# Two layers of attention and a convolutional feed-forward on one core: the rotary key columns taken as one block of high and low halves, and the latents scaled before their transpose

## The chip, the cores and the metric

The kernel runs on one core of one Trainium2 chip. The metric is the device time of one execution in microseconds; lower is better. Three executions of the kernel before took 2210.03, 2210.46 and 2214.27 us, a median of 2210.46 us.

## The reference

For 256 tokens of width 2048 the reference computes two layers, each an attention mixer and a convolutional feed-forward, all in float32. The part around the change is the head of the first layer's mixer:

```python
def mla_mixer(h, positions, mem, w_in, q_norm, w_uq, kv_norm, w_ukv, mem_norm, w_mem_kv, w_o):
    proj = h @ w_in                                     # [256, 2048] @ [2048, 1600]
    q_lat, kv_lat, k_pe, q_mem = proj[..., :512], proj[..., 512:1024], proj[..., 1024:1088], proj[..., 1088:]
    q = (rms_norm(q_lat, q_norm) @ w_uq).reshape(b, s, 12, 192)
    q = concatenate([q[..., :128], rope(q[..., 128:], positions)], axis=-1)
    kv = (rms_norm(kv_lat, kv_norm) @ w_ukv).reshape(b, s, 12, 256)
    k_pe = rope(k_pe[:, :, None, :], positions)         # 64 columns, shared by the 12 heads
    ...
```

Here `h` is `rms_norm(x, a_attn_norm_pre)`, `rms_norm` divides each row by the root of its mean square and multiplies by a gain for each column, and `rope` rotates the two halves of the columns by an angle for each position.

## The kernel before

TensorE multiplies in a format of fewer mantissa bits (fp32r). To keep float32 accuracy every operand is cut in two, a high half (the value rounded) and a low half (the rest), and every product is three matmuls: high by high, low by high, high by low. Activations stand transposed (`xT_hi`, `xT_lo`), with the 2048 columns in 16 chunks of 128 partitions.

**Weights.** SyncE loads one step of weights at a time into a ring of four slots, `w_raw` (L350). ScalarE rounds it into `w_hi` (L1169), VectorE subtracts into `w_lo` (L1708), and TensorE waits for `lo_ready` ahead of each step (L489). SyncE waits for `lo_ready` of four steps ago before it loads a slot again, ScalarE for `step_used`, which TensorE raises at the end of each step. The order on each engine is written out by hand: `splits_to(s)` emits all splits up to step s, and what stands between two of these calls runs between those splits.

**The stage KVLAT.** The first layer's input projection is taken as QLAT (512 query latents, 8 steps), KVLAT (512 key and value latents and the 64 rotary key columns, 16 steps of one chunk, 576 columns of weights) and QMEM (512 memory queries, 8 steps). A chunk of KVLAT is nine matmuls: for each of two blocks of 128 tokens three of 512 columns with the activations stationary, and three for the rotary columns in mode "T", with the 64 weight columns stationary and 256 tokens moving, into `ps[0:64, 7]` (L500 to L512).

**The latents.** At the end of QLAT ScalarE and VectorE scale the two token blocks of PSUM into `lat[:, 0]` (L1292, L1900), ScalarE takes the sums of squares (L1191), and VectorE takes the root's inverse and multiplies an identity matrix by it into `diag` (L1729). After KVLAT TensorE multiplies `lat[:, 0]` by `diag` (`norm_group`, L604), which transposes and scales it at once. The same is done for the key and value latents in `lat[:, 1]`, with `diag_kv`, after QMEM.

**The rotary key columns.** After KVLAT ScalarE copies the 64 x 256 sums to `pe_raw` (L1301). TensorE transposes them after the second step of QMEM (`unrotated_transpose`, L654). VectorE, which waits for that (semaphore `unrotated`), scales them (L1913), rotates them (L1883 to L1890), doubles them (L1895), and only then goes on to the split of the fourth step of QMEM.

Of the kernel before, what the change touches and what calls it, by code (L numbers as in the profile page):

```python
# [22 lines left out]
P = 128  # L23
F32 = mybir.dt.float32
# [3 lines left out]
ALU = mybir.AluOpType  # L28
# [3 lines left out]
S = 256  # L32
# [17 lines left out]
R = 4  # L50
# [94 lines left out]
def program(nc, x_in, mem_in, positions, inv_freq, w, vec, out):  # L145

    with ExitStack() as ctx:
# [46 lines left out]
        diag_kv = at("diag_kv", [P, TT, P], F32, H0 + 24 * KB)  # L194
# [271 lines left out]
        def _(pe):  # L466
# [6 lines left out]
            def product(s0, steps, tile_no, xhi, xlo, parts, width=512, chunks=2, per=0, i=None,  # L473
# [11 lines left out]
                for k, parts_now in turns:  # L485
# [8 lines left out]
                    for c in range(chunks):  # L494
# [5 lines left out]
                        for mode, bank, o0, on, tok, cols in parts_now:  # L500
                            rows = RD if bank >= 4 else P
                            dst = ps[0:rows, bank if bank >= 4 else pair + bank, o0:o0 + on]
# [4 lines left out]
                            pairs = [(a_hi, cols(wh)), (a_hi, cols(wl)), (a_lo, cols(wh))]  # L507
                            if mode == "T":
                                pairs = [(b, a) for a, b in (pairs[0], pairs[2], pairs[1])]
                            for q, (st, mv) in enumerate(pairs):  # L510
                                mm = nc.tensor.matmul(dst, st, mv, start=first and q == 0,  # L511
                                                      stop=last and q == 2, skip_group_check=True)  # L512
# [85 lines left out]
            def norm_group(src, g, diag=diag, tiles=range(TT)):  # L598


                for c in range(2):
                    for t in tiles:
                        f0 = (2 * g + c) * P
                        mm = nc.tensor.matmul(ps[:, 4 + g % 4, 256 * c + P * t:256 * c + P * t + P],  # L604
                                              src[:, t, f0:f0 + P], diag[:, t, :],
                                              start=True, stop=True, skip_group_check=True)
                if TT - 1 in tiles:
                    mm.then_inc(tr_ready, 1)

            def norm_transpose(src, chunks, diag_no, diag=diag):  # L610
                phase_free()
                pe.wait_ge(diag_ready, diag_no)
                for g in range(chunks // 2):
                    if g >= 4:
                        pe.wait_ge(tr_lo, done["N"] + g - 3)
                    norm_group(src, g, diag)
                done["N"] += chunks // 2

            def plain_transpose(src, g, tiles):
# [6 lines left out]
                return mm  # L626

# [238 lines left out]
            def x_group(g):  # L866
                if g >= 4:
# [8 lines left out]
            kpe_parts = [("T", 7, 0, 256, every, (lambda a: a[:, LORA:KVW]))]  # L876
            product(KVLAT, KC, KVLAT_T, xT_hi, xT_lo, n_parts() + kpe_parts, width=KVW, chunks=1)
            norm_transpose(lat[:, 0], 4, 2)
            product(QMEM, DSTEPS, QMEM_T, xT_hi, xT_lo, t_parts(),
                    after=lambda k: k == 1 and unrotated_transpose(6, 0, RD, 1))  # L880
            norm_transpose(lat[:, 1], 4, 3, diag_kv)
# [259 lines left out]
        def _(act):  # L1141
# [175 lines left out]
            to_turn(pe_raw[0:RD, 0, :], ps[0:RD, 7, 0:S])  # L1317
# [352 lines left out]
        def _(dve):  # L1670
# [11 lines left out]
            def split(s, per=0, i=None):  # L1682

                width = 1024
                if i is None and KVLAT <= s < QMEM:
                    width = KVW

# [9 lines left out]
                if i is None and gain_in_split(s):  # L1697
                    for c in range(2):
                        if s < CHUNKED:
# [8 lines left out]
                nc.vector.tensor_tensor(w_lo[:, s % R, 0:width], w_raw[:, s % R, 0:width],  # L1708
                                        w_hi[:, s % R, 0:width].bitcast(F32), ALU.subtract)\
# [23 lines left out]
            def norm(parts, dst=diag):  # L1733
                count["sq"] += 1
                dve.wait_ge(sq_ready, count["sq"])
                sums(parts)
                inverse_std()
                diagonal(dst)
# [159 lines left out]
            def latent_epilogue(k, t, s_end, dst):  # L1898
# [3 lines left out]
                norm(1, dst)  # L1902

            splits_to(KVLAT + AHEAD)
            latent_epilogue(0, QLAT_T, KVLAT, diag)
            splits_to(QMEM + AHEAD)
            latent_epilogue(1, KVLAT_T, QMEM, diag_kv)
# [4 lines left out]
            for t in range(TT):  # L1912
                d = nc.vector.tensor_scalar(raw[:, P * t:P * t + RD], ps[:, 6, P * t:P * t + RD],  # L1913
                                            rstd[:, t:t + 1], None, ALU.mult)
            link(d)
# [472 lines left out]
```

## Time and profile before

| | |
|---|---|
| three executions | 2210.03, 2210.46, 2214.27 us |
| the profiled execution | 2210.6 us, of which the span from first to last instruction is 2208.8 us |
| TensorE clock granted over the span | 0.999 of full speed |
| stage KVLAT | about 131 to 159 us of the span |
| stage QMEM | about 160.5 to 184 us of the span |

Times in rows are microseconds from the start of the span, durations of one instruction nanoseconds. PE is TensorE's matmul, PEld its weight load, DVE VectorE, ACT ScalarE, SPq the queue of SyncE. Matmuls are pipelined: the duration of one is longer than the distance to the next, so the distances between starts tell the pace, not the durations.

### The profile page before, as it was taken

The page shows a single profiled execution, that of the slowest core. Times are in us where ns is not written, and L with a number is a line of the kernel's source. Part 1 is how long each engine was busy: PE and PEld are TensorE (multiplying, and loading weights), DVE is VectorE, ACT ScalarE, POOL GpSimd, SP SyncE. Part 2 cuts the span into 40 slices and gives each one's busy share as a digit, 9 for nine tenths or more (in the row PEclk, how much of TensorE's full clock was granted, in tenths as well). Part 3 has the DMA queues.
Part 4 walks back from the last instruction along what each step waited for, and adds up shares of the span by engine and source line. Part 5 has one row for each costly group of instructions (what it writes and reads, how often), then busy time and mean ns, then how long its engine had stood idle before and what let it go on. Part 6 is the DMA issues. An engine that isn't in the chain of part 4 may idle for free.

```text
span 2208.8 us, 33764 instructions
## 1 busy us (share of the span) xinstructions
PE 2193.8 (99%) x12137; PEld 1909.2 (86%) x12137; DVE 1419.9 (64%) x1897; ACT 1224.1 (55%) x1697; POOL 3.9 (0%) x16
## 2 busy tenths in 40 slices
PE   9999999999999999999999999999999999999998
PEld 9989988888888888888888889888888888888887
DVE  6556656677777776545476667567767776774444
ACT  6655555666565656434465557556655665564443
POOL 0000000000000000000000000000000000000000
PEclk9999999999999999999999999999999999999999
DMA  8565345565656666656655654555565666566664
GB/s 282 180 181 163 115 124 171 182 190 185 197 179 187 192 195 202 202 182 204 195 172 182 197 166 125 182 171 179 188 187 183 195 183 197 179 218 200 192 192 151
DMA packets 208370, 405.61 MB, mean 184 GB/s; under 512 B 12877, under 2 KB 16327, under 8 KB 207519
## 3 DMA queue, kind: packets, MB, share of 16 engines
q1 hardware_dynamic: 207711, 400.29, 58.1%
q0 software_dynamic: 576, 4.19, 0.5%
q8 instruction: 54, 0.88, 0.2%
q14 instruction: 29, 0.24, 0.0%
HBM read 402.34 MB, written 2.10 MB: 183 GB/s over the span
## 4 chain that ended last, share of the span: by engine, by line
PE 98%; DVE 1%; ACT 0%; DMA 0%; issue 0%; DVEq 0%; ACTq 0%
PE ps L511 49%; PE ps L540 29%; PE ps L548 15%; PE ps L981 1%; PE ps L624 1%; PE ps L680 0%; PE ps L764 0%; PE ps L735 0%; PE ps L682 0%; PE ps L644 0%; PE ps L741 0%; DVE w_lo L1702 0%; PE ps L705 0%; DMA gain_rows<-in_gains 0%; PE ps L604 0%; DVE x L2072 0%
## 5 line engine op out<-in xcount | busy, mean ns | idle before, releaser
L1708 DVE TENSOR_TENSOR w_lo<-w_raw,w_hi 128x1024 fp32r<-128x1024 f32 (+1 forms) x636 | 763.3, 1211 | 510.6 <-ACT w_hi L1169 506.1
L1169 ACT ACTIVATE w_hi<-w_raw 128x1024 fp32r<-128x1024 f32 (+1 forms) x636 | 657.4, 1046 | 472.5 <-PE ps L511 337.9
L540 PE MATMUL ps<-xT,w_hi 128*128 128x512 f32 x2816 | 673.4, 391 | 0.1
L540 PEld LDWEIGHTS ps<-xT,w_hi 128*128 128x128 f32 x2816 | 517.1, 188 | 100.2 <-issue 0.4
L548 PEld LDWEIGHTS ps<-xT,w_lo 128*128 128x128 f32 x2816 | 361.6, 191 | 14.3 <-DVE w_lo L1708 0.4
L548 PE MATMUL ps<-xT,w_lo 128*128 128x256 f32 x2816 | 367.4, 283 | 0.0
L511 PE MATMUL ps<-w_hi,hT_hi 128*128 128x512 f32 x704 | 274.0, 389 | 0.0
L511 PE MATMUL ps<-w_hi,hT_lo 128*128 128x512 f32 x704 | 273.9, 389 | 0.0
L511 PE MATMUL ps<-w_lo,hT_hi 128*128 128x512 f32 x704 | 273.9, 389 | 0.0
L1702 DVE SCALAR_TENSOR_TENSOR w_lo<-w_raw,gcol,w_hi 128x512 fp32r<-128x512 f32 x224 | 156.1, 748 | 73.3 <-ACT w_hi L1163 73.2
L511 PE MATMUL ps<-w_hi,xT 128*128 128x512 f32 x640 | 202.2, 391 | 0.0
L1163 ACT ACTIVATE w_hi<-w_raw,gcol 128x512 fp32r<-128x512 f32 x224 | 148.6, 718 | 75.0 <-PE ps L511 63.7
L511 PEld LDWEIGHTS ps<-w_lo,hT_hi 128*128 128x128 f32 x704 | 132.2, 188 | 27.5
L511 PEld LDWEIGHTS ps<-w_hi,hT_hi 128*128 128x128 f32 x704 | 132.2, 188 | 27.4
L511 PEld LDWEIGHTS ps<-w_hi,hT_lo 128*128 128x128 f32 x704 | 132.2, 188 | 27.3
L511 PEld LDWEIGHTS ps<-w_hi,xT 128*128 128x128 f32 x640 | 120.1, 188 | 24.6
L511 PE MATMUL ps<-w_lo,xT 128*128 128x512 f32 x320 | 124.7, 390 | 0.0
L511 PE MATMUL ps<-w_hi,xbT_hi 128*128 128x512 f32 x256 | 100.6, 393 | 0.4 <-DVE w_lo L1702 0.4
L511 PE MATMUL ps<-w_hi,xbT_lo 128*128 128x512 f32 x256 | 99.8, 390 | 0.0
L511 PE MATMUL ps<-w_lo,xbT_hi 128*128 128x512 f32 x256 | 99.7, 389 | 0.0
L1551 ACT ACTIVATE hT_hi<-scratch 128x1024 f32 x22 | 23.4, 1062 | 97.3 <-DVE scratch L2206 97.3
L2196 DVE SCALAR_TENSOR_TENSOR scratch<-u_value,conv,scratch 128x255 f32<-128x255 f32 (+1 forms) x176 | 73.2, 478 | 3.2
(267 smaller groups left out, 2218.6 us busy)
## 6 DMA issues: line engine op xcount, KB each, us to landing
w_raw<-in_ffn_w_in SPq DMA_DIRECT2D x352, 512.0 KB, 4.2
w_raw<-in_ffn_w_out SPq DMA_DIRECT2D x176, 512.0 KB, 4.6
w_raw<-in_shared_w_kv SPq DMA_DIRECT2D x48, 512.0 KB, 3.9
w_raw<-in_a_w_o SPq DMA_DIRECT2D x32, 512.0 KB, 4.6
w_raw<-in_b_w_in SPq DMA_DIRECT2D x32, 512.0 KB, 4.8
w_raw<-in_b_w_o SPq DMA_DIRECT2D x32, 512.0 KB, 4.6
w_raw<-in_a_w_mem_kv SPq DMA_DIRECT2D x16, 512.0 KB, 6.9
w_raw<-in_b_w_mem_kv SPq DMA_DIRECT2D x16, 512.0 KB, 4.6
```

Source lines behind the costliest of these rows:

```text
L511: mm = nc.tensor.matmul(dst, st, mv, start=first and q == 0, stop=last and q == 2, skip_group_check=True)
L540: mm = nc.tensor.matmul(ps[:, base + m4, :].rearrange("p (a n) -> p a n", a=2), w_hi[:, slot, cols], xT[:, :, 2 * k + c, :], start=k == c ...
L548: mm = nc.tensor.matmul(ps[:, base + m4, S:2 * S], w_lo[:, slot, cols], xT_hi[:, 2 * k + c, :], start=False, stop=stop and c == 1, skip_gr ...
L624: mm = nc.tensor.transpose(ps[:, 4 + g % 4, o0:o0 + P], src[:, t, f0:f0 + P], ident[:, :])
L981: mm = nc.tensor.matmul(ps[:, pair + t, :], x_part[:, 2 * k + c, tok_t[t]], w_part[:, slot, 512 * c:512 * (c + 1)], start=t not in started ...
L1163: a = nc.scalar.activation(w_hi[:, s % R, cols], w_raw[:, s % R, cols], ACT.Copy, scale=gcol[:, row:row + 1])
L1169: nc.scalar.activation(w_hi[:, s % R, 0:width], w_raw[:, s % R, 0:width], ACT.Copy)\
L1551: nc.scalar.activation(hT_hi[:, bass.ds(i * 4, 4), :], scratch[:, 1], ACT.Copy).then_inc(h_hi, 1)
L1702: d = nc.vector.scalar_tensor_tensor(out=w_lo[:, s % R, cols], in0=w_raw[:, s % R, cols], scalar=gcol[:, row:row + 1], in1=w_hi[:, s % R, ...
L1708: nc.vector.tensor_tensor(w_lo[:, s % R, 0:width], w_raw[:, s % R, 0:width], w_hi[:, s % R, 0:width].bitcast(F32), ALU.subtract)\
L2196: d = nc.vector.scalar_tensor_tensor(out=c, in0=u, scalar=conv[:, layer, 2 - shift, bass.ds(ch, 1)], in1=c, op0=ALU.mult, op1=ALU.add)
```

## The change

Three things are changed in the first layer; the rest is as it was. In KVLAT, VectorE writes the low half of the 64 rotary columns not into `w_lo` but into `w_hi`, right of the high half (columns 576 to 640), with an instruction of its own. The two halves side by side are one stationary block of 128 columns, which is multiplied by the high and by the low activations (mode "halves"): two matmuls in place of three. The sums of the high half then stand in partitions 0 to 63 of bank 7 and those of the low half in 64 to 127, so that `pe_raw` has 128 rows, and after the transpose VectorE scales both and adds the second to the first. The latents are scaled in place by VectorE (`scale_latent`) and transposed plainly against the identity (`latent_transpose`); `diag_kv` goes. This is the whole difference:

```diff
--- before.py
+++ after.py
@@ -191,7 +191,6 @@
         vm_a = at("vm_a", [P, 2, MH, P], F32, H0 + 68 * KB)
         qpT = at("qpT", [P, AH // 2, S], F32, H0 + 72 * KB)
         kpT = at("kpT", [P, 2, S], F32, H0 + 78 * KB)
-        diag_kv = at("diag_kv", [P, TT, P], F32, H0 + 24 * KB)
 
         xbT_hi = at("xbT_hi", [P, KC, S], F32R, H0)
         xbT_lo = at("xbT_lo", [P, KC, S], F32R, H0 + 16 * KB)
@@ -498,18 +497,22 @@
                         ch = (first_chunk + n_ch) % (steps * chunks)
                         seen = set()
                         for mode, bank, o0, on, tok, cols in parts_now:
-                            rows = RD if bank >= 4 else P
-                            dst = ps[0:rows, bank if bank >= 4 else pair + bank, o0:o0 + on]
+                            dst = ps[:, bank if bank >= 4 else pair + bank, o0:o0 + on]
                             first = n_ch == 0 and bank not in seen
                             seen.add(bank)
                             last = n_ch == steps * chunks - 1
                             a_hi, a_lo = xhi[:, ch, tok], xlo[:, ch, tok]
-                            pairs = [(a_hi, cols(wh)), (a_hi, cols(wl)), (a_lo, cols(wh))]
+                            if mode == "halves":
+                                both = cols(w_hi[:, slot])
+                                pairs = [(both, a_hi), (both, a_lo)]
+                            else:
+                                pairs = [(a_hi, cols(wh)), (a_hi, cols(wl)), (a_lo, cols(wh))]
                             if mode == "T":
                                 pairs = [(b, a) for a, b in (pairs[0], pairs[2], pairs[1])]
                             for q, (st, mv) in enumerate(pairs):
                                 mm = nc.tensor.matmul(dst, st, mv, start=first and q == 0,
-                                                      stop=last and q == 2, skip_group_check=True)
+                                                      stop=last and q == len(pairs) - 1,
+                                                      skip_group_check=True)
                         if between and c + 1 < chunks:
                             between(k)
                     if not single or parts_now[0] is parts[-1]:
@@ -595,27 +598,6 @@
                 if items_done[0]:
                     pe.wait_ge(o_lo, items_done[0])
 
-            def norm_group(src, g, diag=diag, tiles=range(TT)):
-
-
-                for c in range(2):
-                    for t in tiles:
-                        f0 = (2 * g + c) * P
-                        mm = nc.tensor.matmul(ps[:, 4 + g % 4, 256 * c + P * t:256 * c + P * t + P],
-                                              src[:, t, f0:f0 + P], diag[:, t, :],
-                                              start=True, stop=True, skip_group_check=True)
-                if TT - 1 in tiles:
-                    mm.then_inc(tr_ready, 1)
-
-            def norm_transpose(src, chunks, diag_no, diag=diag):
-                phase_free()
-                pe.wait_ge(diag_ready, diag_no)
-                for g in range(chunks // 2):
-                    if g >= 4:
-                        pe.wait_ge(tr_lo, done["N"] + g - 3)
-                    norm_group(src, g, diag)
-                done["N"] += chunks // 2
-
             def plain_transpose(src, g, tiles):
 
                 for c in range(2):
@@ -624,6 +606,14 @@
                         mm = nc.tensor.transpose(ps[:, 4 + g % 4, o0:o0 + P], src[:, t, f0:f0 + P],
                                                  ident[:, :])
                 return mm
+
+            def latent_transpose(src, scaled_no):
+
+                phase_free()
+                pe.wait_ge(diag_ready, scaled_no)
+                for g in range(2):
+                    plain_transpose(src, g, range(TT)).then_inc(tr_ready, 1)
+                done["N"] += 2
 
             def x_transpose(g, tiles):
 
@@ -873,12 +863,12 @@
             product(QLAT, DSTEPS, QLAT_T, xT_hi, xT_lo, n_parts(),
                     late=[(k, None, tr_lo, base_n + k + 1) for k in range(DSTEPS)])
 
-            kpe_parts = [("T", 7, 0, 256, every, (lambda a: a[:, LORA:KVW]))]
+            kpe_parts = [("halves", 7, 0, 256, every, (lambda a: a[:, LORA:KVW + RD]))]
             product(KVLAT, KC, KVLAT_T, xT_hi, xT_lo, n_parts() + kpe_parts, width=KVW, chunks=1)
-            norm_transpose(lat[:, 0], 4, 2)
+            latent_transpose(lat[:, 0], 2)
             product(QMEM, DSTEPS, QMEM_T, xT_hi, xT_lo, t_parts(),
-                    after=lambda k: k == 1 and unrotated_transpose(6, 0, RD, 1))
-            norm_transpose(lat[:, 1], 4, 3, diag_kv)
+                    after=lambda k: k == 1 and unrotated_transpose(6, 0, P, 1))
+            latent_transpose(lat[:, 1], 3)
             rope_transpose(6, [rot[:, P * t:P * (t + 1)] for t in range(TT)], 1)
             qpe_blocks = [rot[:, P * t:P * (t + 1)] for t in range(TT)]
             for j in range(6):
@@ -1314,7 +1304,7 @@
             latent_epilogue(0, QLAT_T, KVLAT)
             splits_to(QMEM + AHEAD)
             latent_epilogue(1, KVLAT_T, QMEM)
-            to_turn(pe_raw[0:RD, 0, :], ps[0:RD, 7, 0:S])
+            to_turn(pe_raw[:, 0, :], ps[:, 7, 0:S])
             split_transposes(4, [(GAIN_ROWS["q_norm"], latq_hi)])
             splits_to(UQ + AHEAD)
             act.wait_ge(step_used, UQ)
@@ -1681,10 +1671,6 @@
 
             def split(s, per=0, i=None):
 
-                width = 1024
-                if i is None and KVLAT <= s < QMEM:
-                    width = KVW
-
                 if i is not None or s >= CHUNKED:
                     dve.wait_ge(hi_ready, val(s + 1, per, i))
                 if i is None and UQ <= s < UKV:
@@ -1705,8 +1691,15 @@
                             op0=ALU.mult, op1=ALU.subtract)
                     d.then_inc(lo_ready, 1)
                     return
-                nc.vector.tensor_tensor(w_lo[:, s % R, 0:width], w_raw[:, s % R, 0:width],
-                                        w_hi[:, s % R, 0:width].bitcast(F32), ALU.subtract)\
+                if i is None and KVLAT <= s < QMEM:
+                    for dst, cols in ((w_lo[:, s % R, 0:LORA], slice(0, LORA)),
+                                      (w_hi[:, s % R, KVW:KVW + RD], slice(LORA, KVW))):
+                        d = nc.vector.tensor_tensor(dst, w_raw[:, s % R, cols],
+                                                    w_hi[:, s % R, cols].bitcast(F32), ALU.subtract)
+                    d.then_inc(lo_ready, 1)
+                    return
+                nc.vector.tensor_tensor(w_lo[:, s % R, :], w_raw[:, s % R, :],
+                                        w_hi[:, s % R, :].bitcast(F32), ALU.subtract)\
                     .then_inc(lo_ready, 1)
 
             def splits_to(s):
@@ -1730,12 +1723,15 @@
                                                 ALU.mult)
                 d.then_inc(diag_ready, 1)
 
-            def norm(parts, dst=diag):
+            def scale_latent(k):
                 count["sq"] += 1
                 dve.wait_ge(sq_ready, count["sq"])
-                sums(parts)
+                sums(1)
                 inverse_std()
-                diagonal(dst)
+                for t in range(TT):
+                    d = nc.vector.tensor_scalar(lat[:, k, t, :], lat[:, k, t, :],
+                                                nrm[:, 4 + t:5 + t], None, ALU.mult)
+                d.then_inc(diag_ready, 1)
 
             def split_transposes(chunks, targets, following=None, start=3):
 
@@ -1895,16 +1891,16 @@
                     d = nc.vector.tensor_copy(rows[:, :, width:2 * width], rows[:, :, 0:width])
                 d.then_inc(rope_ready, 1)
 
-            def latent_epilogue(k, t, s_end, dst):
+            def latent_epilogue(k, t, s_end):
                 dve.wait_ge(step_used, s_end)
                 nc.vector.tensor_scalar(lat[:, k, 1, :], ps[:, 2 * (t % 2) + 1, :], rstd[:, 1:2], None,
                                         ALU.mult).then_inc(pair_dve, 1)
-                norm(1, dst)
+                scale_latent(k)
 
             splits_to(KVLAT + AHEAD)
-            latent_epilogue(0, QLAT_T, KVLAT, diag)
+            latent_epilogue(0, QLAT_T, KVLAT)
             splits_to(QMEM + AHEAD)
-            latent_epilogue(1, KVLAT_T, QMEM, diag_kv)
+            latent_epilogue(1, KVLAT_T, QMEM)
             split_transposes(4, [(GAIN_ROWS["q_norm"], latq_hi, latq_lo)])
             nc.vector.memset(kpT[RD:P, 0, :], 0.0)
             nc.vector.memset(kpT[0:RD, 1, :], 0.0)
@@ -1912,6 +1908,11 @@
             for t in range(TT):
                 d = nc.vector.tensor_scalar(raw[:, P * t:P * t + RD], ps[:, 6, P * t:P * t + RD],
                                             rstd[:, t:t + 1], None, ALU.mult)
+            link(d)
+            for t in range(TT):
+                d = nc.vector.scalar_tensor_tensor(
+                    out=raw[:, P * t:P * t + RD], in0=ps[:, 6, P * t + RD:P * (t + 1)],
+                    scalar=rstd[:, t:t + 1], in1=raw[:, P * t:P * t + RD], op0=ALU.mult, op1=ALU.add)
             link(d)
             rotate(unrotated, 1, P, RD, 0, RD // 2, twice=True)
             splits_to(UQ + AHEAD)
```

TensorE, one chunk of KVLAT. `ps` is the accumulator, `xT` the activations; left of the comma after the arrow are the operands of the matmul, and the last number is its output. Before:

```order
L511 MATMUL ps<-w_hi,xT 128x512
L511 MATMUL ps<-xT,w_hi 64x256 x2
L511 MATMUL ps<-xT,w_lo 64x256
L511 MATMUL ps<-w_hi,xT 128x512
L511 MATMUL ps<-w_lo,xT 128x512
L511 MATMUL ps<-w_hi,xT 128x512 x2
```

And after, at the same place:

```order
L513 MATMUL ps<-w_hi,xT 128x512
L513 MATMUL ps<-xT,w_hi 128x256 x2
L513 MATMUL ps<-w_hi,xT 128x512
L513 MATMUL ps<-w_lo,xT 128x512
L513 MATMUL ps<-w_hi,xT 128x512 x2
```

The three matmuls that write 64 partitions became two that write 128; the six of 512 columns around them stay.

VectorE at the start of KVLAT, from the first three splits through the query latents to the further splits (`nrm` is the sum of squares and the root's inverse). Before:

```order
L1708 TENSOR_TENSOR w_lo<-w_raw,w_hi 128x576 x3
L1900 TENSOR_SCALAR lat<-ps,rstd 128x512
L1719 TENSOR_REDUCE nrm<-ssp 128x2
L1725 RECIPROCAL nrm<-nrm 128x2
L1729 TENSOR_SCALAR diag<-ident,nrm 128x128 x2
L1708 TENSOR_TENSOR w_lo<-w_raw,w_hi 128x576 x13
```

After:

```order
L1697 TENSOR_TENSOR w_lo<-w_raw,w_hi 128x512
L1697 TENSOR_TENSOR w_hi<-w_raw,w_hi 128x64
L1896 TENSOR_SCALAR lat<-ps,rstd 128x512
L1712 TENSOR_REDUCE nrm<-ssp 128x2
L1718 RECIPROCAL nrm<-nrm 128x2
L1732 TENSOR_SCALAR lat<-lat,nrm 128x512 x2
L1697 TENSOR_TENSOR w_lo<-w_raw,w_hi 128x512
L1697 TENSOR_TENSOR w_hi<-w_raw,w_hi 128x64
```

Each of the 16 splits became two instructions, and the two scalings ahead of the fourth split have 512 columns in place of 128.

VectorE in QMEM, from the wait for the transposed rotary columns to the split of QMEM's fourth step (`scratch` holds them). Before:

```order
L1910 MEMSET kpT 64x256
L1913 TENSOR_SCALAR scratch<-ps,rstd 128x64 x2
L1883 TENSOR_TENSOR scratch<-scratch,sine 128x2x32
L1886 TENSOR_TENSOR scratch<-scratch,sine 128x2x32
L1887 TENSOR_TENSOR scratch<-scratch,cosine 128x2x32
L1888 TENSOR_TENSOR scratch<-scratch,cosine 128x2x32
L1889 TENSOR_TENSOR scratch<-scratch 128x2x32
L1890 TENSOR_TENSOR scratch<-scratch 128x2x32
L1895 COPY scratch<-scratch 128x2x64
L1708 TENSOR_TENSOR w_lo<-w_raw,w_hi 128x1024 x5
```

After:

```order
L1906 MEMSET kpT 64x256
L1909 TENSOR_SCALAR scratch<-ps,rstd 128x64 x2
L1913 SCALAR_TENSOR_TENSOR scratch<-ps,rstd,scratch 128x64 x2
L1879 TENSOR_TENSOR scratch<-scratch,sine 128x2x32
L1882 TENSOR_TENSOR scratch<-scratch,sine 128x2x32
L1883 TENSOR_TENSOR scratch<-scratch,cosine 128x2x32
L1884 TENSOR_TENSOR scratch<-scratch,cosine 128x2x32
L1885 TENSOR_TENSOR scratch<-scratch 128x2x32
L1886 TENSOR_TENSOR scratch<-scratch 128x2x32
L1891 COPY scratch<-scratch 128x2x64
L1701 TENSOR_TENSOR w_lo<-w_raw,w_hi 128x1024 x5
```

Two instructions came in between the scaling and the rotation, ahead of the five splits.

## Rows read from the trace of the kernel before

**Rows 1.** The profile's page: busy time of engines, and the chain that ended last.

```profile
PE 2193.8 (99%) x12137; PEld 1909.2 (86%) x12137; DVE 1419.9 (64%) x1897; ACT 1224.1 (55%) x1697; POOL 3.9 (0%) x16
...
PE 98%; DVE 1%; ACT 0%; DMA 0%; issue 0%; DVEq 0%; ACTq 0%
```

**Rows 2.** Timeline of TensorE in KVLAT: start, length, instruction; two merged are x2.

```profile
135.97 0.40 PE L511 MATMUL ps<-xT,w_hi 128*64 128x256 f32 x2
136.21 0.28 PE L511 MATMUL ps<-xT,w_lo 128*64 128x256 f32 x1
136.32 0.40 PE L511 MATMUL ps<-w_hi,xT 128*128 128x512 f32 x1
...
137.71 0.40 PE L511 MATMUL ps<-xT,w_hi 128*64 128x256 f32 x2
```

**Rows 3.** Instructions grouped by form: rotary matmuls and weight loads, busy us, mean ns.

```profile
L511 PEld LDWEIGHTS ps<-xT,w_hi 128*128 128x128 f32 x128 | 19.9, 192 | 0.2 <-DVE w_lo L1708 0.2
...
L511 PE MATMUL ps<-xT,w_hi 128*64 128x256 f32 x32 | 6.3, 280 | 0.0
...
L511 PEld LDWEIGHTS ps<-xT,w_hi 128*64 128x64 f32 x32 | 4.3, 134 | 2.1
```

**Rows 4.** The chain that ended last in time order: start, length, pieces, 85 to 100.

```profile
95.84 0.44 PE ps L624 x4
```

**Rows 5.** The same chain, 158 to 190: the latents' transposes and QMEM.

```profile
159.02 1.78 PE ps L604 x16
160.80 5.74 PE ps L511 x48
166.55 0.26 PE ps L654 x2
```

**Rows 6.** Timeline of VectorE and TensorE: query latents, then KVLAT's fourth step.

```profile
134.28 0.48 DVE L1729 TENSOR_SCALAR diag<-ident,nrm 128x128 f32<-128x128 f32 x2
134.68 2.09 DVE L1708 TENSOR_TENSOR w_lo<-w_raw,w_hi 128x576 fp32r<-128x576 f32 x3
136.21 0.19 PEld L511 LDWEIGHTS ps<-w_hi,xT 128*128 128x128 f32 x1
```

**Rows 7.** VectorE's instructions grouped by form, all before 260 us.

```profile
L1708 DVE TENSOR_TENSOR w_lo<-w_raw,w_hi 128x576 fp32r<-128x576 f32 x16 | 11.9, 757 | 14.4 <-ACT w_hi L1169 14.4
L1692 DVE TENSOR_TENSOR w_lo<-w_raw,w_hi 128x512 fp32r<-128x512 f32 x12 | 8.2, 686 | 4.7 <-ACT w_hi L1155 4.7
...
L1748 DVE SCALAR_TENSOR_TENSOR latk_lo<-ps,gcol,latk_hi 128x256 fp32r<-128x256 f32 x4 | 1.8, 480 | 1.1 <-ACT latk_hi L1204 1.1
...
L1900 DVE TENSOR_SCALAR lat<-ps,rstd 128x512 f32<-128x512 f32 x2 | 1.5, 748 | 1.2 <-PE ps L511 1.2
...
L1769 DVE TENSOR_SCALAR turns<-turns 128x384 f32<-128x384 f32 x1 | 0.4, 360 | 0.0
...
L1889 DVE TENSOR_TENSOR scratch<-scratch 128x64 f32<-128x64 f32 x1 | 0.2, 225 | 0.0
```

**Rows 8.** Timeline 162.9 to 170.3: rotary columns, then QMEM's fourth step.

```profile
166.48 0.33 PE L654 MATMUL ps<-ident,pe_raw 64*128 64x64 f32 x2
166.85 0.48 DVE L1913 TENSOR_SCALAR scratch<-ps,rstd 128x64 f32<-128x64 f32 x2 [1.11 <-PE ps L654]
167.36 0.22 DVE L1883 TENSOR_TENSOR scratch<-scratch,sine 128x64 f32<-128x64 f32 x1
...
168.57 2.35 DVE L1708 TENSOR_TENSOR w_lo<-w_raw,w_hi 128x1024 fp32r<-128x1024 f32 x2
...
169.59 0.28 PE L511 MATMUL ps<-xT,w_lo 128*128 128x256 f32 x1
169.84 0.30 PEld L511 LDWEIGHTS ps<-xT,w_hi 128*128 128x128 f32 x2 [0.18 <-DVE w_lo L1708]
169.84 0.51 PE L511 MATMUL ps<-xT,w_hi 128*128 128x256 f32 x2
```

**Rows 9.** Loads of weights issued from 148 to 162 us.

```profile
DMA to landing us min/median/max: 3.6/4.5/4.8
```

## The prediction

> **What bounds the kernel now.** I read the profile's page first. TensorE is busy in 99% of the span, and the chain that ended last runs on TensorE for 98% of it [rows 1]. So a matmul taken from TensorE shortens the run by the distance it takes in the stream, unless a wait comes in its place, and work on VectorE counts only where TensorE waits for it. The timeline of TensorE in the stage KVLAT is next. One chunk goes from 135.97 to 137.71, 1.73 to 1.74 us for nine matmuls with no gap; its three rotary matmuls go from 135.97 to 136.32, 0.35 us [rows 2]. Last comes the place where VectorE is late already. In QMEM TensorE's load at 169.84 was idle 0.18 us before it, released by VectorE's split, which begins at 168.57 as the end of a chain that starts when TensorE's two small transposes of the rotary columns are done: TensorE 166.48, VectorE 166.85, 167.36, then 168.57 [rows 8]. A change that lengthens this chain is paid on TensorE at once.
>
> **Rotary matmuls in KVLAT.** Three matmuls of 256 columns with 64 stationary columns go, two of 256 with 128 stationary columns come. Three take 0.35 us now, 0.117 each. The new form, 128 stationary and 256 moving, is that of QMEM: 48 in 5.74 us, 0.120 each [rows 5]. Two make 0.24, so a chunk gives back 0.105, and 16 chunks 1.7 us. Bounds: a whole slot of 0.12 in each chunk gives 1.9 us. From below, the weight loads, which take 192 ns with 128 columns against 134 with 64 [rows 3], could come to light: two at 0.192 are 0.38 a chunk, 0.03 to 0.04 more than the three cost now, and 16 chunks lose 0.6 us. I take 1.7, because in the 5.74 us of QMEM exactly such loads are hidden behind exactly such matmuls.
>
> The Trainium skill has a rule that speaks against this edit: in "TensorE: Matmul & The Clock Gate", section "LDWEIGHTS (loading the stationary operand)", a load costs by its columns, not by its rows, so two loads of 128 are more loading than three of 64. The trace agrees on the load itself (58 ns more for 64 columns more), but the pace in QMEM shows it hidden; where it weren't, the sum would turn from a gain to a loss, which is a rival below.
>
> **VectorE in KVLAT.** Each split was 757 ns for 576 columns; now 512 columns (686, the same operation on 512) and 64 (225) [rows 7]. Two queued instructions overlap by about 0.08 (the pair at 134.28 spans 0.48 with 0.28 each [rows 6]), so 0.82 or 0.83, 0.07 more. In a stage with 1.6 us a chunk for 0.83 us of work this is covered by TensorE's matmuls, with one exception, the start of the stage. There VectorE scales the query latents between the third and fourth split. Now the two multiplications of the identity take 0.48, and the fourth split begins at 134.68 and ends 0.76 later, at 135.44; TensorE wants it at the load of 136.21 [rows 6]: 0.77 to spare. In place of 128 columns come 512. A multiplication in SBUF by a scalar takes 360 ns for 384 columns [rows 7], at most 0.48 for 512; two come to 0.88, 0.40 more. With the 0.07 of the split VectorE is ready 0.47 later. TensorE comes 3 x 0.105 = 0.32 earlier. 0.79 against 0.77: the cover is just used up, and with the some 0.05 us that a waiting load starts after its release (split begun 168.57, 1.22 long by its pace in the pair of 2.35, load at 169.84 [rows 8]) I put a stall of 0.1 us here. Bounds: 0 if the scaling is quicker; if it runs at the 748 ns that 512 columns from PSUM take [rows 7], 0.94 more for the two, 0.6 us of stall. The nearer row is that of SBUF. The fifth split comes 0.83 after the fourth and TensorE 1.63 after, so it isn't repeated.
>
> **Scaling and transposes of the latents.** Neither needs a new wait: the query latents are scaled around 135 and used at 159, the key latents around 163 and used at 184. On the key side the scaling's 0.4 us falls into VectorE's idle 1.11 us ahead of 166.85 [rows 8]; without that cover it would be added to the chain below. On TensorE 32 matmuls with the diagonal become 32 transposes. 16 of the first take 1.78, 0.111 each [rows 5], four of the second 0.44, 0.110 each [rows 4]: 0.03 us in all, bounds 0 and 0.1. The wider transposes of the rotary columns (0.26 for two of 64 [rows 5], 0.22 for two at that 0.110) cost nothing. ScalarE's copy has twice the partitions and the same columns: nothing.
>
> The Trainium skill lets one expect more here. "TensorE: Matmul & The Clock Gate", section "Terms", calls the transpose mode four times faster for FP32. By that 32 transposes at a quarter of the distance would give 2.7 us; the trace disagrees, since transposes of the same shape show 0.110.
>
> **The rotary chain in QMEM.** It gets one more pair on 64 columns out of PSUM, and a wait between the pairs. The pair that is there goes from 166.85 to 167.36 with its wait, 0.51 [rows 8]. The new pair reads PSUM and SBUF; the nearest row is the same operation on 256 columns, 480 ns [rows 7], which shrinks toward 0.28 at 64. So 0.5 us, from 0.4 to 0.9 (two at the full 480 less the overlap). Since TensorE already waits here, and both start at the same transposes, all of it is stall: +0.5 us. The four splits behind it are needed one each 2.9 us and take 1.2, so nothing later is late. SyncE's next load moves by the same 0.5 and goes through the ring with chunks in hand.
>
> **The sum.** -1.7 - 0.03 + 0.1 + 0.5 = -1.1 us. The profiled execution took 2210.6 us, 1.8 more than its span of 2208.8; it becomes 2209.5 with a span of 2207.7. The median shown, 2210.46, is 0.14 below the profiled one, so I predict 2209.4. The rest of the program is moved as a whole: at 99% busy there is no slack that would swallow a microsecond, and none that would give more.
>
> **The rivals.**
> - *The rotary chain is hidden.* The new pair costs nothing: -1.6, 2208.9. For it: VectorE idles 1.11 us ahead of the chain. Against: the idle time lies before TensorE's transposes, the chain behind them, and TensorE is shown waiting at its end. 8%.
> - *Weight loads come to light (the other side).* Place: each of the 16 chunks, at the change from rotary matmuls to the next; price +0.6 in place of -1.7, with the stalls +1.2: 2211.7, slower. It decides from a pair that takes over 0.35 us. The loads' length speaks for it, QMEM's pace against it. 5%.
> - *The fourth split is really late.* Scaling at PSUM's rate, stall 0.6: 2209.9. For it: the spare time is just used up. Against: the SBUF row. 8%.
> - *Transposes at a quarter of the distance.* -1.1 - 2.6: 2206.8. Only the page speaks for it; the transposes in the trace don't. 3%.
> - *Loads of weights come late.* KVLAT's chunks are shorter, so QMEM's first loads must land in 4 x 1.63 - 1.7 = 4.8 us to be there when ScalarE turns to them; they land in 3.6 to 4.8 [rows 9], and TensorE wants them three chunks later still. Hidden; 2%, with half a microsecond lost, 2209.9.
>
> **How the numbers follow.** 74% for the forecast, whose own range with the bounds of its terms is 2209.0 to 2210.4. Three executions of before spread over 4 us upward, and the medians of a few runs move by some tenths; with the rivals and that, 8 in 10 is 2208.2 to 2211.8, which leaves out the quarter-distance case and single high medians. What a measurement can tell from no change is about 0.2%, 4.4 us. None of the cases reaches it in either direction except by scatter: same 0.89, faster 0.07 (the forecast's sign and the 3% case help), slower 0.04.
>
> **What would show it.** A chunk of KVLAT at 1.63 us in place of 1.735, with its rotary pair 0.24 us. VectorE's fourth split ending near 135.9, TensorE idle 0.1 or less there. In QMEM the wait of TensorE for the split grown from 0.18 to about 0.7, with 0.51 more between the first scaling and the rotation. 16 transposes in 1.76 us. KVLAT's and QMEM's distances alike elsewhere. I am wrong if the pair takes over 0.3 us, if the wait in QMEM stays near 0.2, or if places outside 131 to 187 us differ by more than some tenths.

## The result, and the profile after

The changed kernel took 2207.56 us (median of 20 runs, 2207.01 to 2210.27), the kernel before 2210.6 us (20 runs, 2210.03 to 2214.27). The ratio is 0.9986 with a 95% interval of 0.9981 to 0.9992: about 3 us less, where 1.1 less was forecast, and below the range of 2208.2 to 2211.8. The profiled execution has this span and this work, from the profile's page:

```profile
span 2205.9 us, 33718 instructions
...
PE 2190.3 (99%) x12105; PEld 1907.2 (86%) x12105; DVE 1422.1 (64%) x1915; ACT 1224.2 (55%) x1697; POOL 3.9 (0%) x16
```

TensorE still bounds the kernel. It has 32 records fewer than in [rows 1]. Sixteen of them are the rotary matmuls, one for each chunk. The other sixteen belong to no step of the forecast. They show in the chain that ended last, the transposes of the key latents after QMEM (start, length, pieces):

```profile
167.77 14.66 PE ps L513 x120
182.43 0.87 PE ps L606 x8
```

The group that was 16 pieces in 1.78 us [rows 5] is 8 pieces in 0.87. It is the same for the query latents, where the start of the first transpose (157.22) and that of QMEM's first matmul (158.01) are 0.79 apart. That alone is 1.8 us for the two groups.

The rotary matmuls in KVLAT, timeline of TensorE (start, length, instruction), to be laid beside [rows 2]:

```profile
134.24 0.40 PE L513 MATMUL ps<-xT,w_hi 128*128 128x256 f32 x2
...
135.86 0.40 PE L513 MATMUL ps<-xT,w_hi 128*128 128x256 f32 x2
136.09 0.47 PE L513 MATMUL ps<-w_hi,xT 128*128 128x512 f32 x1
136.40 0.39 PE L513 MATMUL ps<-w_lo,xT 128*128 128x512 f32 x1
```

A chunk now takes 1.62 us, the rotary pair 0.23. The matmul at 136.09 is the first of the fourth chunk; the next follows 0.31 after it and not 0.23 to 0.24, a stall of 0.07. VectorE's timeline at that place:

```profile
134.40 0.88 DVE L1732 TENSOR_SCALAR lat<-lat,nrm 128x512 f32<-128x512 f32 x2
...
135.19 0.69 DVE L1697 TENSOR_TENSOR w_lo<-w_raw,w_hi 128x512 fp32r<-128x512 f32 x1
...
135.79 0.22 DVE L1697 TENSOR_TENSOR w_hi<-w_raw,w_hi 128x64 fp32r<-128x64 f32 x1
```

ScalarE's split of the eighth chunk's weights, whose load waits for VectorE's fourth split (in brackets the wait ahead of it, and what ended it). Before, and after:

```profile
138.32 0.69 ACT L1169 ACTIVATE w_hi<-w_raw 128x576 fp32r<-128x576 f32 x1 [1.05 <-PE ps L511]
...
138.88 0.69 ACT L1159 ACTIVATE w_hi<-w_raw 128x576 fp32r<-128x576 f32 x1 [1.84 <-DMA w_raw<-in_a_w_in]
```

The fourth split ends at 136.01, against 135.44 worked out from [rows 6]. Counted from the first rotary matmul (132.51 before, 132.62 after) it ends 0.46 later, and ScalarE's split of the eighth chunk begins 0.45 later, because the load between them is issued later. Of the 1.84 us that ScalarE waits for that load not all is new, since before it waited 1.05 there for TensorE. It has chunks in hand, so TensorE doesn't feel it.

QMEM, timeline of TensorE and VectorE, to be laid beside [rows 8]:

```profile
163.72 0.28 PE L513 MATMUL ps<-xT,w_lo 128*128 128x256 f32 x1
...
163.84 0.38 PE L644 MATMUL ps<-ident,pe_raw 128*128 128x128 f32 x2
...
163.98 0.48 PE L513 MATMUL ps<-xT,w_hi 128*128 128x256 f32 x2
...
164.17 0.27 DVE L1906 MEMSET kpT<- 64x256 f32 x1
...
164.36 0.38 DVE L1909 TENSOR_SCALAR scratch<-ps,rstd 128x64 f32<-128x64 f32 x2
...
164.78 0.48 DVE L1913 SCALAR_TENSOR_TENSOR scratch<-ps,rstd,scratch 128x64 f32<-128x64 f32 x2
...
165.29 0.23 DVE L1879 TENSOR_TENSOR scratch<-scratch,sine 128x64 f32<-128x64 f32 x1
...
166.50 4.62 DVE L1701 TENSOR_TENSOR w_lo<-w_raw,w_hi 128x1024 fp32r<-128x1024 f32 x4
...
167.76 0.30 PEld L513 LDWEIGHTS ps<-xT,w_hi 128*128 128x128 f32 x2 [0.87 <-DVE w_lo L1701]
```

The last matmul ahead of the small transposes was, before:

```profile
166.27 0.28 PE L511 MATMUL ps<-xT,w_lo 128*128 128x256 f32 x1
```

The added pair takes 0.51 from 164.78 to 165.29, and TensorE's wait grew from 0.18 to 0.87 us. From the last matmul ahead of the small transposes to the load of the fourth step it is 163.72 to 167.76, 4.04 us, against 166.27 to 169.84, 3.57, before: the step costs 0.47 more. VectorE's idle time ahead of the scaling, 1.11 us in [rows 8], is gone: VectorE comes late to the transposed columns. The chain that ended last goes back from its memsets over its splits to a load:

```profile
150.95 5.09 DMA w_raw<-in_a_w_in
```

Whether this load cost TensorE anything is asked below, with e9, e11 and e12.

**How runs are compared below.** The part ahead of KVLAT varies: its first rotary matmul started between 131.93 and 133.14 us in the fourteen profiles. So beside the median I give the distance from that matmul to the last matmul of the program (line of `ps<-w_hi,hT_lo`). Before it is 2200.64 - 132.51 = 2068.13 us, after 2197.74 - 132.62 = 2065.12: 3.01 less. Each distance comes from one profile. Kernels that were expected to be alike in it differ by up to 0.1 us (e2 and e3 by 0.06, e4 and the changed kernel by 0.09).

| run | median us | ratio (95%) | distance against before, us |
|---|---|---|---|
| after | 2207.56 | 0.9986 (0.9981 to 0.9992) | -3.01 |
| e1_transposes_only | 2208.7 | 0.9994 (0.9985 to 1.0003) | 2198.45 - 132.10: -1.78 |
| e2_halves_only | 2209.14 | 0.9994 (0.9985 to 1.0003) | 2199.26 - 132.43: -1.30 |
| e3_matmul_identity | 2209.17 | 0.9994 (0.9985 to 1.0003) | 2199.31 - 132.42: -1.24 |
| e4_matmul_fp32r | 2207.4 | 0.9986 (0.9977 to 0.9996) | 2197.41 - 132.38: -3.10 |
| e5_two_narrow | 2208.09 (1 run) | | 2198.16 - 131.93: -1.90 |
| e6_split_first | 2206.51 | 0.9981 (0.9972 to 0.9990) | 2196.74 - 132.57: -3.96 |
| e7_both_splits_first | 2206.3 | 0.9982 (0.9973 to 0.9991) | 2196.31 - 132.17: -3.99 |
| e8_narrow_turn | 2207.61 (1 run) | | 2197.63 - 132.23: -2.73 |
| e9_no_pair | 2208.06 (1 run) | | 2198.13 - 133.14: -3.14 |
| e10_all_early | 2206.34 | 0.9982 (0.9973 to 0.9991) | 2196.14 - 132.04: -4.03 |
| e11_memsets_early | 2207.27 | 0.9986 (0.9977 to 0.9995) | 2197.56 - 132.39: -2.96 |
| e12_memsets_early_no_pair | 2206.66 | 0.9983 (0.9973 to 0.9992) | 2196.59 - 132.07: -3.61 |

### The profile page after: what moved, and what is told of

It is laid out like the page before. It is cut to its first block, busy times and chain, and to the rows that moved or that the text cites. A ratio compares the mean times of both kernels' runs of the same rounds, so it can differ in the third digit from the quotient of the medians.

```text
span 2205.9 us, 33718 instructions
## 1 busy us (share of the span) xinstructions
PE 2190.3 (99%) x12105; PEld 1907.2 (86%) x12105; DVE 1422.1 (64%) x1915; ACT 1224.2 (55%) x1697; POOL 3.9 (0%) x16
## 4 chain that ended last, share of the span: by engine, by line
PE 98%; DVE 1%; ACT 1%; DMA 0%; issue 0%; DVEq 0%; ACTq 0%
PE ps L513 48%; PE ps L543 29%; PE ps L551 15%; PE ps L606 1%; PE ps L971 1%; PE ps L670 0%; PE ps L754 0%; PE ps L725 0%; PE ps L672 0%; PE ps L634 0%; PE ps L731 0%; DMA w_raw<-in_a_w_in 0%; DVE w_lo L1688 0%; PE ps L695 0%; DMA gain_rows<-in_gains 0%
## 5 line engine op out<-in xcount | busy, mean ns | idle before, releaser
L1701 DVE TENSOR_TENSOR w_lo<-w_raw,w_hi 128x1024 fp32r<-128x1024 f32 x620 | 751.5, 1223 | 493.1 <-ACT w_hi L1159 488.8
```

The source lines that it names most:

```text
L1701: nc.vector.tensor_tensor(w_lo[:, s % R, :], w_raw[:, s % R, :], w_hi[:, s % R, :].bitcast(F32), ALU.subtract)\
```

## The experiments: where the missing 1.9 us came from

**One part alone.** e1 is the kernel before with the latents' part of the change.

```diff
-            norm_transpose(lat[:, 0], 4, 2)
+            latent_transpose(lat[:, 0], 2)
-            norm_transpose(lat[:, 1], 4, 3, diag_kv)
+            latent_transpose(lat[:, 1], 3)
-                norm(1, dst)
+                scale_latent(k)
```

> The kernel before with the latents scaled in place and transposed plainly, and the rotary columns as they were. Theory A (a float32 matmul is two passes in TensorE's stream, a transpose one): each group of latents takes 0.87 to 0.91 us in place of 1.78, so the span is 1.8 us shorter, about 2207.0 us, ratio 0.9992. The wait in QMEM stays near 0.2 us. Theory B (a transpose costs what the matmul with the diagonal costs, as forecast, and the change's gain came from the rotary columns): 0.0 to 0.1 us.

The chain in e1, query latents:

```profile
158.62 0.87 PE ps L624 x8
```

The distance fell by 1.78, the group of 16 pieces became 8, and the wait in QMEM is 0.17 us: theory A. e2 is the other part alone.

```diff
-                    plain_transpose(src, g, range(TT)).then_inc(tr_ready, 1)
+                            mm = nc.tensor.matmul(ps[:, 4 + g, 256 * c + P * t:256 * c + P * t + P],
+                                                  src[:, t, f0:f0 + P], dg[:, t, :],
+                                                  start=True, stop=True, skip_group_check=True)
...
-                    d = nc.vector.tensor_scalar(lat[:, k, t, :], lat[:, k, t, :],
-                                                nrm[:, 4 + t:5 + t], None, ALU.mult)
+                diagonal(diag if k == 0 else diag_kv)
```

> The changed kernel with the latents transposed by the matmul with the scaled diagonal, as before. Theory A: the rotary columns give back 1.75 us in KVLAT and lose 0.5 in QMEM, so 1.2 us less than before, span 2207.6, ratio 0.9994; each latent group still 1.78 us. Theory B: the whole gain is here, 2.9 us, span 2205.9.

The chain in e2, query latents:

```profile
157.13 1.79 PE ps L620 x16
```

Its distance fell by 1.30, 1.2 expected, and the wait in QMEM is 0.87 us as after. The parts add up: 1.78 + 1.30 = 3.08 against 3.01 together.

**Transpose mode or number format.** e3 multiplies the scaled latents by the identity as an ordinary matmul.

```diff
-                    plain_transpose(src, g, range(TT)).then_inc(tr_ready, 1)
+                            mm = nc.tensor.matmul(ps[:, 4 + g, 256 * c + P * t:256 * c + P * t + P],
+                                                  src[:, t, f0:f0 + P], ident[:, :],
+                                                  start=True, stop=True, skip_group_check=True)
```

> The changed kernel, with the scaled latents multiplied by the identity as an ordinary float32 matmul in place of the transpose mode. Theory A: eight matmuls show 16 records again and take 1.78 us a group, so 1.8 us more than the changed kernel, span 2207.7. Theory B: the same as the changed kernel, 2205.9.

The group of these matmuls in e3, from the groups by line (busy, mean ns of one, idle time ahead):

```profile
L618 PE MATMUL ps<-ident,lat 128*128 128x128 f32 x32 | 3.9, 275 | 0.0
```

The chain in e3, query latents:

```profile
157.20 1.79 PE ps L618 x16
```

The program issues 8 matmuls for each group of latents, and there are 16 records for each. 1.77 of the 3.01 us are lost. So the diagonal itself is not what costs, nor is the identity free: an ordinary float32 matmul shows two records and takes two slots. e4 does the same in fp32r.

```diff
-        lat = at("lat", [P, 2, TT, LORA], F32, H0 + 16 * KB)
+        lat = at("lat", [P, 2, TT, LORA], F32R, H0 + 16 * KB)
+        ident_r = at("ident_r", [P, P], F32R, H0 + 24 * KB)
-                    plain_transpose(src, g, range(TT)).then_inc(tr_ready, 1)
+                                                  src[:, t, f0:f0 + P], ident_r[:, :],
```

> The changed kernel, with the latents held in the shorter format fp32r (their low mantissa bits are lost) and multiplied by an identity in that format as an ordinary matmul. If the second pass belongs to float32 operands (theory A), eight records and about 0.9 us a group, span as the changed kernel's, 2205.9 within 0.2. If it belongs to every matmul that isn't in transpose mode, 16 records and 1.8 us, span 2207.7.

The chain in e4, query latents:

```profile
157.15 0.85 PE ps L619 x8
```

8 records, 0.85 us a group, the whole gain. The second slot belongs to float32 operands of an ordinary matmul; both the shorter format and the transpose mode take one. A matmul with only one of its operands in float32 wasn't tried.

**What the wide stationary block costs.** e5 keeps 64 stationary columns and drops the third matmul.

```diff
+                            if bank >= 4:
+                                pairs = pairs[:2]
```

> The kernel before, with two of the three rotary matmuls of KVLAT, both with 64 stationary columns (the high activations by the low weights are left out). It tells what 128 stationary columns cost against 64. Theory A (loads hidden): a chunk takes 1.61 to 1.63 us, like the changed kernel's 1.62. Rival (the wider load is partly paid): 1.55 to 1.60.

TensorE's timeline in e5, the rotary matmuls of two neighbouring chunks:

```profile
140.00 0.40 PE L513 MATMUL ps<-xT,w_hi 128*64 128x256 f32 x2
...
141.61 0.40 PE L513 MATMUL ps<-xT,w_hi 128*64 128x256 f32 x2
```

A chunk takes 1.61 us, with 128 columns 1.62. The wider load is hidden; the rival of exposed loads fell.

## The experiments: the wait in QMEM

**The split first.** e6 moves the split of QMEM's fourth step on VectorE ahead of the rotary columns.

```diff
+            splits_to(QMEM + AHEAD + 1)
             nc.vector.memset(kpT[RD:P, 0, :], 0.0)
```

> The changed kernel, with the split of QMEM's fourth step moved ahead of the rotary columns on VectorE. Theory A (the rotary chain stands between TensorE and this split): the wait of 0.87 us goes, span 2205.1, 0.75 to 0.9 us less than the changed kernel. Rival (VectorE or the loads are late as a whole, by the late load of KVLAT): the wait only moves to a neighbouring step, span 2205.6 or more.

The rest of QMEM after the small transposes, the chain of before and then that of e6:

```profile
166.81 17.69 PE ps L511 x144
...
164.18 17.28 PE ps L513 x144
```

These 144 matmuls to the end of QMEM take 17.28 us in e6, whose trace shows no wait of TensorE's loads for a split between 100 and 260 us. In the kernel before, with its wait of 0.18 and its transposes of 64 rows (see e8), they took 0.41 more. The distance is 0.95 below that of the changed kernel, where 0.75 to 0.9 was expected.

**The chain's parts.** e9 takes the added pair away.

```diff
-            for t in range(TT):
-                d = nc.vector.scalar_tensor_tensor(
-                    out=raw[:, P * t:P * t + RD], in0=ps[:, 6, P * t + RD:P * (t + 1)],
-                    scalar=rstd[:, t:t + 1], in1=raw[:, P * t:P * t + RD], op0=ALU.mult, op1=ALU.add)
-            link(d)
```

> The changed kernel without the added pair of instructions on VectorE (the low half's product isn't added). Theory A: the wait of TensorE for QMEM's fourth step falls from 0.87 to 0.3 or 0.4 us, and the span from 2205.9 to 2205.4. Rival (the wait comes from late loads): it stays over 0.7.

The timeline of VectorE and TensorE's weight load in e9:

```profile
165.14 0.27 DVE L1906 MEMSET kpT<- 64x256 f32 x1
165.33 0.34 DVE L1909 TENSOR_SCALAR scratch<-ps,rstd 128x64 f32<-128x64 f32 x2
...
166.91 2.35 DVE L1701 TENSOR_TENSOR w_lo<-w_raw,w_hi 128x1024 fp32r<-128x1024 f32 x2
...
168.18 0.30 PEld L513 LDWEIGHTS ps<-xT,w_hi 128*128 128x128 f32 x2 [0.77 <-DVE w_lo L1701]
```

A miss for theory A: the wait fell from 0.87 to 0.77 only. TensorE's small transposes had started at 164.37, but VectorE was at the memsets until 165.33. It was late there because ScalarE had waited longer for loads in this execution, and VectorE does its splits after ScalarE's. The load that the chain goes back to in e9, and ScalarE's timeline:

```profile
151.48 5.54 DMA w_raw<-in_a_w_in
...
155.76 1.06 ACT L1159 ACTIVATE w_hi<-w_raw 128x1024 fp32r<-128x1024 f32 x1 [1.55 <-DMA w_raw<-in_a_w_in]
```

In the changed kernel this wait was 1.10, at 154.78. Counted from the first rotary matmul (133.14 in e9), the load landed 23.88 us in, against 23.42 in the changed kernel, and VectorE's scaling began 32.19 in, against 31.74: 0.45 later. e11 and e12 separate the two, with the memsets moved ahead of KVLAT, where VectorE idles.

```diff
+            nc.vector.memset(kpT[RD:P, 0, :], 0.0)
+            nc.vector.memset(kpT[0:RD, 1, :], 0.0)
             splits_to(KVLAT + AHEAD)
```

> The changed kernel with only the two memsets moved ahead of KVLAT, which gives VectorE 0.7 us of slack ahead of the rotary columns. Theory A (e9 gained little because late loads brought VectorE late to the transposed columns): VectorE waits for TensorE again there, and TensorE's wait is 0.75 to 0.9 us, from the rotary chain alone.

The same timeline in e11:

```profile
164.05 0.47 DVE L1909 TENSOR_SCALAR scratch<-ps,rstd 128x64 f32<-128x64 f32 x2 [0.22 <-PE ps L644]
...
167.56 0.30 PEld L513 LDWEIGHTS ps<-xT,w_hi 128*128 128x128 f32 x2 [0.88 <-DVE w_lo L1701]
```

e12 is e11 without the pair, the edits of e9 and e11 together.

> As e11, without the added pair on VectorE (the low half's product isn't added). Theory A: against e11 the wait falls by the 0.5 us of the pair, to 0.3 or 0.4. Rival (the wait is set by late loads): within 0.15 us of e11.

The same timeline in e12:

```profile
163.72 0.48 DVE L1909 TENSOR_SCALAR scratch<-ps,rstd 128x64 f32<-128x64 f32 x2 [0.30 <-PE ps L644]
...
166.70 0.30 PEld L513 LDWEIGHTS ps<-xT,w_hi 128*128 128x128 f32 x2 [0.35 <-DVE w_lo L1701]
```

With VectorE waiting for TensorE again, the pair's price shows in full: 0.88 against 0.35, 0.53 us. (The distances are 0.65 apart, 0.12 more than these rows explain.) The whole wait of the changed kernel is there with VectorE in time: counted from the first rotary matmul, the load of the fourth step comes at 35.17 in e11 and 35.14 in the changed kernel. So in the profiled execution of that kernel the late loads cost nothing; in e9 they had filled what the pair left free, 0.47 us of distance against e12. Whether they cost some tenths in other executions of the changed kernel stays open: its median is 0.29 above that of e11, but the two come from different sets of runs, and the median of before also differs by 0.18 between these sets (2210.6 and 2210.42).

**64 or 128 rows.** e8 turns 64 rows in the small transposes in place of 128, in the changed kernel.

```diff
-                    after=lambda k: k == 1 and unrotated_transpose(6, 0, P, 1))
+                    after=lambda k: k == 1 and unrotated_transpose(6, 0, RD, 1))
...
-                    out=raw[:, P * t:P * t + RD], in0=ps[:, 6, P * t + RD:P * (t + 1)],
+                    out=raw[:, P * t:P * t + RD], in0=ps[:, 6, P * t:P * t + RD],
```

> The changed kernel, with the rotary columns' two transposes 64 x 64 as before (VectorE adds the high half's product twice, the low half's is left out). If transposes of 64 rows leave a gap in TensorE's stream that those of 128 do not, the distance from the matmul before them to the second after them is 0.69 us, as in the kernel before; if not, 0.46 as in the changed kernel.

TensorE's timeline in e8:

```profile
163.34 0.28 PE L513 MATMUL ps<-xT,w_lo 128*128 128x256 f32 x1
163.55 0.33 PE L644 MATMUL ps<-ident,pe_raw 64*128 64x64 f32 x2
163.81 0.50 PE L513 MATMUL ps<-xT,w_hi 128*128 128x256 f32 x2
```

Two merged matmuls of 0.28 in 0.50 put the second at 163.81 + 0.50 - 0.28 = 164.03, 0.69 behind 163.34; in the changed kernel it is 163.98 + 0.48 - 0.28 = 164.18, 0.46 behind 163.72. The small turns with 64 rows cost TensorE 0.23 us more than those with 128: 0.09 of it lies ahead of the first transpose (0.21 behind the matmul before it, against 0.12) and 0.12 between the first transpose and the first matmul behind them (0.26 against 0.14).

The distance of e8 is 0.28 above that of the changed kernel, but these 0.23 are not the reason, since TensorE waits behind them for the chain in both. The chain in e8 goes back to a late load once more:

```profile
150.56 5.42 DMA w_raw<-in_a_w_in
```

Counted from the first rotary matmul (132.23), it landed 23.75 us in, 0.33 later than in the changed kernel, VectorE's scaling began 0.32 later, and the load of the fourth step came 0.28 later. Here the late load was paid.

**The best order.** e7 adds the same move in KVLAT to e6, e10 the memsets of e11.

```diff
                 inverse_std()
+                if k == 0:
+                    splits_to(KVLAT + AHEAD + 1)
```

> As e6, and in KVLAT the fourth split also goes ahead of the scaling of the query latents. Theory A: the small stall at KVLAT's fourth chunk (0.07 us) goes and the following loads start earlier, span 2204.8, 0.1 us less than e6. Rival (the later split is what holds the loads back, and it costs more than the stall shows): 0.3 us or more less than e6, or a chunk pace in KVLAT below 1.62 us.

> As e7, with the two memsets of kpT moved ahead of KVLAT. TensorE doesn't wait there any more in e6, so theory A expects no change against e7 (within 0.1 us of span); if VectorE is still behind in QMEM, 0.1 to 0.3 us less.

The stall at the fourth chunk is gone in e7 (its first two matmuls start at 135.64 and 135.87, 0.23 apart), but as times neither can be told from e6: 0.03 and 0.07 us of distance, medians within 0.21 us of each other. ScalarE's waits for loads stay, 1.38 us once in e7, so they don't hang on the fourth split alone. All three, at 2206.3 to 2206.5 us, lie below both kernels; against the changed one, whose median comes from other runs, it is some 1.0 to 1.3 us.

## Why the prediction was wrong

**The step that failed** is the price of the latents' transposes: "16 of the first take 1.78, 0.111 each [rows 5], four of the second 0.44, 0.110 each [rows 4]: 0.03 us in all". The 1.78 is right, and so is the 0.110. The 16 are not 16 matmuls. `norm_group` (L604) has two chunks by two blocks of tokens and is called for two groups: 8 matmuls for the query latents and 8 for the key latents, each with two records in the trace. A matmul with the diagonal takes 0.223 us, a transpose 0.109, and 16 of them save 1.8 us, not 32 of them 0.03. So the sum put at nothing a term as large as that of the rotary matmuls. e1, e2, e3 and e4 show it from four sides. The count of the program stood beside the rows all the time; I took the number of records for it.

The same step made a rival too unlikely. Transposes at a quarter of the distance had 3% and 2.6 us. The rule of the Trainium skill behind it ("TensorE: Matmul & The Clock Gate", section "Terms": four times faster for FP32) pointed the right way; the runs show twice, 0.87 against 1.78 us. I turned it down because transposes of the same shape show 0.110, but to refute it I needed the distance of one float32 matmul, and I had halved that.

**Point by point.**
- *Rotary matmuls, -1.7: right.* From the first rotary matmul to the last one of the stage, 15 chunks, it was 158.51 - 132.51 = 26.00 and is 156.99 - 132.62 = 24.37, with the stall of 0.07 in it: 0.11 a chunk, 1.8 for 16. Exposed weight loads: refuted by e5.
- *The fourth split, +0.1: right*, 0.07. The scaling in SBUF took its 0.88 us, and the end at 136.01 is where the sum put it.
- *The latents' transposes, -0.03: wrong*, -1.8.
- *The rotary chain, +0.5: right.* 0.47 from end to end, 0.53 by e11 against e12. The forecast of the wait, 0.7, was short of 0.87, because I had taken TensorE's side as fixed, and it came 0.23 earlier with turns of 128 rows. It doesn't change the sum, since TensorE waited for the chain in any case.
- *Loads come late, 2%: it happened, and cost nothing here.* QMEM's loads landed in up to 5.4 us where 4.8 were in hand; ScalarE waited 1.10 us at 154.78, and the cover of VectorE ahead of the rotary columns went. "Here" is the profiled execution: in those of e8 and e9 the same lateness was paid, with 0.28 and 0.47 us. So 2% was too small a chance.

With the transposes at -1.8 in its place my sum is -1.7 - 1.8 + 0.1 + 0.5 = -2.9, and the span became 2.9 us shorter. The direction was right; the size and the range were wrong. The forecast also took 0.2% as what a measurement can tell from no change. The change is 0.14%, less than that, and still the interval of twenty runs on each side, 0.9981 to 0.9992, lies wholly below 1.

## What to carry to other kernels

Count what an operation issues in the program before dividing a busy time by the number of its records: where the trace has twice as many records as the code has matmuls, each takes two slots, as here. In a kernel bound by TensorE, ordinary float32 matmuls that only move or scale data are worth replacing by transposes with the scaling on an engine that has time. Where TensorE already waits at the end of a chain on another engine, put the work that it waits for ahead of that chain before the chain is lengthened: one line moved gave back 0.95 us.

## What the runs showed of the hardware that was not expected

- A float32 matmul of 128 x 128 by 128 columns leaves two records and takes 0.223 us in a stream (1.79 for 8); the same in fp32r 0.106 (0.85 for 8), in transpose mode 0.109 (0.87 for 8).
- Two transposes of 64 rows between matmuls of 128 rows cost TensorE 0.23 us more than two of 128 rows. The timelines show 0.09 of it on the way in and 0.12 on the way out; why it is so wasn't tried.
- A split that ended 0.46 us later moved the load behind it: ScalarE began the split of that load 0.45 us later and waited 1.84 us for it, where before it had waited 1.05 there for TensorE. The loads of KVLAT issued between 131 and 147 us landed in 2.7 to 3.9 us (median 2.8) before and in 2.8 to 3.9 (median 3.2) after. The fourth split isn't the whole cause: with it moved ahead again, in e7, ScalarE still waits 1.38 us there for the load.
- With the same code up to that point, one load of QMEM took 5.09 us in the changed kernel, 5.42 in e8 and 5.54 in e9, and VectorE came to the rotary columns 0.32 and 0.45 us later in the two than in the changed kernel.
